# The first weight chunk of a two-layer decoder kernel: both tiles as fp32 products, loaded in 256 KB pieces on two queues

## The chip, the core and the metric

One core of one Trainium2 chip runs the whole kernel as one program. The metric is the device time of one execution in microseconds: 598.82 us is the median of three runs of the kernel before (598.73 to 599.18).

## The reference, cut to what matters

The model is a two-layer decoder trunk on 256 tokens of width 1024, all in float32. Layer 0 projects the input once, `x @ w_in`, and splits the columns: queries of a sparse attention (A), a shared key/value latent `c_kv` of 128 columns, queries, a key and weights of a small indexer, and queries, keys and values of a stick-breaking attention (B). The indexer picks 64 keys for each query.

```python
q_a, c_kv, q_idx, k_idx, w_idx, q_b, k_b, v_b = jnp.split(x @ w_in, cuts, axis=-1)
o_a = dsa_attention(q_a, rms_norm(c_kv, kv_norm), q_idx, k_idx, w_idx * IDX_HEADS ** -0.5, w_uk, w_uv)
o_b = stick_breaking_attention(q_b, k_b, v_b)
o = jnp.concatenate([o_a, o_b], axis=-1)
h = layer_norm(DEEPNORM_ALPHA * h + o @ w_out, ...)
h = layer_norm(DEEPNORM_ALPHA * h + (silu(h @ w_gate) * (h @ w_up)) @ w_down, ...)
```

Layer 1 has another attention in the same frame. The change touches only the first two tiles of `x @ w_in`: the tile of the indexer's key and weights (`k_idx`, `w_idx`), and the tile of the latent (`c_kv`).

## The kernel before

All weights come as a stream of chunks of 1 MB, 128 partitions by 2048 numbers. Chunks of the usual kind are loaded as two halves of 512 KB by SyncE (SP) into a ring of two `raw` buffers. ScalarE (ACT) rounds each half to fp32r, the high part (`split_hi_half`, into `whi`), and VectorE (DVE) subtracts to get the low part (`split_lo_half`, into `wlo`). The profile calls both `wboth`. TensorE (PE) then does three fp32r passes for each product, high by high, high by low and low by high (`HT_PASSES`), each of 128 by 256. The transposed input is `hT` (in the memory of `v`, so the profile names it `v`), with its two parts `hThi` and `hTlo` (`hTs` in the profile). A contraction over 1024 has eight tiles of 128 (`KT`).

Chunk 0 is special. It is loaded into the memory of `kT` (name `first`), and holds two tiles side by side, columns 0 to 1023 for the key and weights tile and 1024 to 2047 for the latent tile. The key and weights tile is done as plain fp32 products straight from the loaded data: 8 products, each of which the profile shows as two MATMUL records. The latent tile is done like all others, from high and low parts that ACT and DVE make by quarters (`first_quarter`), in 24 fp32r products. Ahead of the first data, PE multiplies zeros (`WARM` times, 512 columns each).

What sets the order at the start is code written out by hand for each engine. PE: zeros, key and weights tile, latent tile, chunk 1 (line 1396 and the function `cols_out`), the first half of chunk 2, transposes and the indexer's scores, and so on; from there to the end PE goes through the chunks in turn. ACT: the high parts of `hT`, of the latent tile, of chunks 1 and 2, then the copies of the first results out of PSUM, which end in `proj_evac` 1. SP issues the loads; from chunk 3 on each waits until DVE has finished with the half that it overwrites (`wlo_ready`). POOL issues the constants' load when the second half of chunk 1 has landed, and three small loads of weights when chunk 2 has.

PE reads chunk c when `wlo_ready` is 2c. The first half of chunk 2 also waits for `proj_evac` 1, and the indexer's scores for `proj_evac` 2.

Of the kernel before, what the change touches and what calls it, by code (L numbers as in the profile page):

```python
# [21 lines left out]
F32 = mybir.dt.float32  # L22
F32R = mybir.dt.float32r
ALU = mybir.AluOpType
# [3 lines left out]
P = 128  # L28
D = 1024
S = 256  # L30
KT = D // P
# [9 lines left out]
CW = 2048  # L41
# [19 lines left out]
def build(nc, x, xT, stream, w_uk, w_uv, kv_norm, ln_rows, consts, out):  # L61
    with ExitStack() as ctx:
# [3 lines left out]
        def sem(name):  # L66
            return ctx.enter_context(nc.semaphore(name))
# [4 lines left out]
        whi, wlo = wboth[:, :, 0], wboth[:, :, 1]  # L72
# [10 lines left out]
        hT = v[:].rearrange("p t (k s) -> p (t k) s", s=S)  # L83
# [11 lines left out]
        bank = [ctx.enter_context(nc.psum_tensor(f"bank{b}", [P, 512], F32)) for b in range(8)]  # L95
# [12 lines left out]
        crawT = dsel[:, 0:S]  # L108


        first = kT[:].rearrange("p k s -> p (k s)")
        FIRST = [slice(i * CW // 2, (i + 1) * CW // 2) for i in range(2)]
        QUARTER = [slice(i * CW // 4, (i + 1) * CW // 4) for i in range(4)]
# [19 lines left out]
        xT_loaded = [sem(f"xT_loaded{i}") for i in range(2)]  # L133
        first_loaded = [sem(f"first_loaded{i}") for i in range(2)]
        first_hi, first_lo = sem("first_hi"), sem("first_lo")
# [3 lines left out]
        hThi_ready, hTlo_ready = sem("hThi_ready"), sem("hTlo_ready")  # L139
# [71 lines left out]
        WARM = 10  # L211
# [65 lines left out]
        def _(sp):  # L277
            half = (slice(0, HW), slice(HW, CW))
            sp.dma_start(first[:, FIRST[0]], stream[0][:, FIRST[0]]).then_inc(first_loaded[0], 16)
            sp.dma_start(hT[:, 4:8], xT[:, 4:8]).then_inc(xT_loaded[1], 16)  # L280
            sp.dma_start(first[:, FIRST[1]], stream[0][:, FIRST[1]]).then_inc(first_loaded[1], 16)
# [17 lines left out]
            for c in range(L1_IN - 1, L1_OUT + 1):  # L299
                for j in range(2):  # L300
                    sp.wait_ge(wlo_ready, 2 * (c - RAW) + j - 1)
                    at = L1_IN + L1_ORDER[c - L1_IN] if L1_IN <= c < L1_OUT else c
# [70 lines left out]
        def _(act):  # L373
            def split_hi_half(c, j, i=0):
                act.wait_ge(raw_loaded[c % RAW][j], 16 * (c // RAW + c % RAW) + 16 * (RING // RAW) * i)
                nc.scalar.copy(whi[:, c % RING, j * HW:(j + 1) * HW], raw[:, c % RAW, j * HW:(j + 1) * HW]  # L376
                               ).then_inc(whi_ready, 1)
# [76 lines left out]
            act.dma_start(hT[:, 0:4], xT[:, 0:4]).then_inc(xT_loaded[0], 16)  # L454
            act.preload_act_table_set("natural_log_exp_and_others")
            def first_quarter(i):
                act.wait_ge(first_loaded[i // 2], 16)
                nc.scalar.copy(whi[:, 0, QUARTER[i]], first[:, QUARTER[i]]).then_inc(first_hi, 1)

            for b in range(4):  # L460
                act.wait_ge(xT_loaded[b // 2], 16)
                nc.scalar.copy(hThi[:, 2 * b:2 * b + 2], hT[:, 2 * b:2 * b + 2]).then_inc(hThi_ready, 1)
            first_quarter(2)
            first_quarter(3)
            split_hi(1)
            split_hi_half(2, 0)
            act.wait_ge(chunk_used, 1)
            nc.scalar.copy(crawT, bank[4][:, S:2 * S])
# [4 lines left out]
            split_hi_half(2, 1)  # L473
# [249 lines left out]
            for s in range(SLOTS1):  # L723
                q, half = FILL1[s]
# [24 lines left out]
        def _(dve):  # L749
# [128 lines left out]
            def first_quarter(i):  # L878
                dve.wait_ge(first_hi, i - 1)
                nc.vector.tensor_tensor(wlo[:, 0, QUARTER[i]], first[:, QUARTER[i]],  # L880
                                        whi[:, 0, QUARTER[i]].bitcast(F32), ALU.subtract).then_inc(first_lo, 1)

# [4 lines left out]
            first_quarter(2)  # L887
            first_quarter(3)
# [5 lines left out]
            for i in range(I_HEADS):  # L894
                dve.wait_ge(relu_done, i + 1)
                for t in range(2):
                    w = wq_i[:, t, i:i + 1]
# [232 lines left out]
        def _(pe):  # L1130
            mm = nc.tensor.matmul
# [239 lines left out]
            pe.wait_ge(first_loaded[0], 16)  # L1371
            for k in range(KT):
                if k % 4 == 0:
                    pe.wait_ge(xT_loaded[k // 4], 16)
                mm(bank[4][:, 0:S], first[:, k * P:(k + 1) * P], hT[:, k, :], start=(k == 0), stop=(k == KT - 1))
            for q in range(2):
                ks = range(4 * q, 4 * q + 4)
                for j, (w, a) in enumerate(HT_PASSES):
                    if j == 0:
                        pe.wait_ge(hThi_ready, 2 * q + 2)  # L1380
                        pe.wait_ge(first_hi, q + 1)
                    elif j == 1:
                        pe.wait_ge(hTlo_ready, 2 * q + 2)
                    else:
                        pe.wait_ge(first_lo, q + 1)
                    for k in ks:
                        last = mm(bank[4][:, S:2 * S], w[:, 0, (KT + k) * P:(KT + k + 1) * P], a[:, k, :],
                                  start=(k == 0 and j == 0), stop=(k == KT - 1 and j == 2))
            last.then_inc(chunk_used, 1)
            for j, (w, a) in enumerate(HT_PASSES):  # L1390
                if j == 0:
                    pe.wait_ge(whi_ready, 1)
                elif j == 2:
                    pe.wait_ge(wlo_ready, 1)
                for k in range(KT):
                    mm(bank[5][:, 0:S], w[:, 1, k * P:(k + 1) * P], a[:, k, :], start=(k == 0 and j == 0),
                       stop=(k == KT - 1 and j == 2))
# [472 lines left out]
```

## Time and profile before

| what | value |
|---|---|
| median of three runs | 598.82 us |
| the profiled execution's own time | 598.94 us |
| its span, first to last instruction | 597.2 us |
| PE busy | 589.1 us (99%) |
| PE weight load busy | 505.7 us (85%) |
| DVE busy | 424.4 us (71%) |
| ACT busy | 342.3 us (57%) |
| HBM read | 107.94 MB, 183 GB/s over the span |

The profile shows one execution. A line of instructions has the source line, the engine, the operation, what it writes and what it reads. PE's busy time is not PE at its peak, since records of pipelined matmuls overlap. The chain that ended last is followed back from the last instruction, and its entries give where the time of the end comes from. 1.74 us of the profiled execution lie outside its span.

### The profile page before, as it was taken

To read this page: it belongs to the slowest core of one execution; us is meant where nothing else is said; L and a number is where in the kernel's file an instruction comes from. 1 tells how busy PE (TensorE), PEld (TensorE's weight loads), DVE (VectorE), ACT (ScalarE), POOL (GpSimd) and SP (SyncE) were. 2 spreads that over 40 slices of the span, in tenths; PEclk is the share of its full clock that TensorE was granted. 3 is DMA by queue.
4 is the path that set the end of the run, shared out by engine and by line. 5 is a ranking of instruction groups with operands and counts; after the bars stand their busy time and mean duration, and the time that the engine had idled before them with its cause. 6 is when DMAs were issued, how large, how long until landed. Compare 5 with 4: busy or idle time off the path is not lost.

```text
span 597.2 us, 9595 instructions
## 1 busy us (share of the span) xinstructions
PE 589.1 (99%) x3354; PEld 505.7 (85%) x3354; DVE 424.4 (71%) x697; ACT 342.3 (57%) x645; POOL 26.6 (4%) x49
## 2 busy tenths in 40 slices
PE   8999999999999999999999999999999999999995
PEld 7988888888888888888888888888888888888885
DVE  4699877876776556655887888768677666665637
ACT  5776986456655544554556767645565555555530
POOL 1111111100000000000010000002000000000000
PEclk9999999999999999999999999999999999999999
DMA  8755437286676565564447543662767655555401
GB/s 309 265 179 194 142 124 245 91 291 202 223 223 207 193 205 181 182 205 140 143 148 270 180 141 117 205 207 80 237 217 234 210 202 165 185 186 189 140 1 70
DMA packets 30112, 109.43 MB, mean 183 GB/s; under 512 B 3376, under 2 KB 3376, under 8 KB 29952
## 3 DMA queue, kind: packets, MB, share of 16 engines
q1 hardware_dynamic: 28368, 102.25, 51.9%
q0 software_dynamic: 1568, 6.23, 3.4%
q10 hardware_dynamic: 144, 0.52, 0.2%
q8 instruction: 21, 0.34, 0.2%
q14 instruction: 11, 0.09, 0.0%
HBM read 107.94 MB, written 1.05 MB: 183 GB/s over the span
## 4 chain that ended last, share of the span: by engine, by line
PE 98%; DMA 1%; DVE 0%; DVEq 0%; issue 0%; ACT 0%; ACTq 0%
PE bank L1244 27%; PE bank L1152 24%; PE bank L1158 13%; PE bank L1694 5%; PE bank L1522 3%; PE bank L1698 3%; PE bank L1145 2%; PE bank L1222 2%; PE bank L1197 2%; PE bank L1198 2%; PE bank L1204 2%; PE bank L1339 1%; PE bank L1350 1%; PE bank L1330 1%; PE bank L1526 1%; PE bank L1501 1%
## 5 line engine op out<-in xcount | busy, mean ns | idle before, releaser
L753 DVE TENSOR_TENSOR wboth<-raw,wboth 128x1024 fp32r<-128x1024 f32 x190 | 225.3, 1223 | 44.5 <-ACT wboth L376 43.6
L376 ACT CAST wboth<-raw 128x1024 fp32r<-128x1024 f32 x190 | 191.2, 1047 | 21.6 <-DMA raw<-stream_in 20.8
L1152 PE MATMUL bank<-hTs,wboth 128*128 128x512 f32 x640 | 152.2, 390 | 0.0
L1244 PE MATMUL bank<-wboth,oThi 128*128 128x512 f32 x468 | 150.1, 392 | 0.0
L1152 PEld LDWEIGHTS bank<-hTs,wboth 128*128 128x128 f32 x640 | 118.8, 188 | 23.7
L1244 PEld LDWEIGHTS bank<-wboth,oThi 128*128 128x128 f32 x468 | 88.0, 188 | 18.3 <-issue 0.7
L1244 PE MATMUL bank<-wboth,oTlo 128*128 128x512 f32 x234 | 91.3, 390 | 0.0
L1158 PEld LDWEIGHTS bank<-hTs,wboth 128*128 128x128 f32 x640 | 81.9, 191 | 3.0
L1158 PE MATMUL bank<-hTs,wboth 128*128 128x256 f32 x640 | 83.2, 283 | 0.0
L1244 PEld LDWEIGHTS bank<-wboth,oTlo 128*128 128x128 f32 x234 | 44.0, 188 | 8.1
L654 ACT COPY kT<-bank 128x256 f32<-128x256 f32 x40 | 14.8, 371 | 58.8 <-PE bank L1158 58.7
L661 ACT CAST oThi<-scratch 128x256 fp32r<-128x256 f32 x40 | 16.3, 406 | 41.1 <-DVE scratch L1058 41.1
L1050 DVE TENSOR_TENSOR kT<-bank,kT 128x256 f32<-128x256 f32 x40 | 16.8, 420 | 31.5 <-ACT kT L654 31.5
L1053 DVE TENSOR_TENSOR kT<-bank,kT 128x256 f32<-128x256 f32 x40 | 17.0, 425 | 30.4 <-ACT kT L659 30.4
L657 ACT ACTIVATE scratch<-kT 128x256 f32<-128x256 f32 x40 | 16.7, 418 | 36.2 <-DVE kT L1050 36.2
L1694 PE MATMUL bank<-hTs,wboth 128*128 128x512 f32 x128 | 32.6, 395 | 0.0
L1061 DVE TENSOR_TENSOR oTlo<-scratch,oThi 128x256 fp32r<-128x256 f32 x40 | 17.0, 425 | 18.9 <-ACT oThi L661 18.9
L1694 PEld LDWEIGHTS bank<-hTs,wboth 128*128 128x128 f32 x128 | 23.0, 189 | 5.1 <-issue 1.0
L1058 DVE TENSOR_TENSOR scratch<-scratch,kT 128x256 f32<-128x256 f32 x40 | 17.0, 426 | 4.4 <-DVE kT L1053 1.5
L1197 PE MATMUL bank<-wboth,hTs 128*128 128x512 f32 x48 | 18.8, 392 | 0.0
L1198 PE MATMUL bank<-wboth,hTs 128*128 128x512 f32 x48 | 18.7, 391 | 0.0
L1698 PEld LDWEIGHTS bank<-hTs,wboth 128*128 128x128 f32 x128 | 17.4, 190 | 1.3
(189 smaller groups left out, 635.1 us busy)
## 6 DMA issues: line engine op xcount, KB each, us to landing
raw<-stream_in SPq DMA_DIRECT2D x190, 512.0 KB, 4.9
qT<-ln_rows_in POOLq DMA_DIRECT2D x8, 512.0 KB, 5.1
kT<-stream_in SPq DMA_DIRECT2D x2, 512.0 KB, 6.2
h<-x_in POOLq DMA_DIRECT2D x1, 1024.0 KB, 5.0
out<-h SPq DMA_DIRECT2D x4, 256.0 KB, 2.1
v<-xT_in ACTq DMA_DIRECT2D x1, 512.0 KB, 5.1
v<-xT_in SPq DMA_DIRECT2D x1, 512.0 KB, 6.6
dist<-consts_in POOLq DMA_DIRECT2D x1, 384.0 KB, 3.5
```

Source lines behind the costliest of these rows:

```text
L376: nc.scalar.copy(whi[:, c % RING, j * HW:(j + 1) * HW], raw[:, c % RAW, j * HW:(j + 1) * HW]).then_inc(whi_ready, 1)
L753: nc.vector.tensor_tensor(wlo[:, c % RING, cols], raw[:, c % RAW, cols], whi[:, c % RING, cols].bitcast(F32), ALU.subtract).then_inc(wlo_r ...
L1053: nc.vector.tensor_tensor(uful[:, t % 2], bank[tile_bank(t) + 1][:, 0:S], uful[:, t % 2], ALU.add).then_inc(usum_ready, 1)
L1058: nc.vector.tensor_tensor(aful[:, t % 2], sgate[:, t % 2], uful[:, t % 2], ALU.mult).then_inc(amul_ready, 1)
L1152: mm(dst[:], whi[:, slot, off + k * P:off + (k + 1) * P], hTs[:, k].rearrange("p j s -> p (j s)"), start=(k == 0), stop=False)
L1158: last = mm(dst[:, 0:S], wlo[:, slot, off + k * P:off + (k + 1) * P], hThi[:, k, :], start=False, stop=(k == KT - 1))
L1197: mm(dst, hThi[:, k, toks], whi[:, slots, cols], start=(k == 0), stop=False)
L1198: mm(dst, hThi[:, k, toks], wlo[:, slots, cols], start=False, stop=False)
L1244: last = mm(bank[4 + 2 * t + a][:], o[:, kts[j], t * P:(t + 1) * P], w[:, c % RING, j * D + a * 512:j * D + (a + 1) * 512], start=(start a ...
L1522: mm(dst[:], whi[:, c % RING, at + k * P:at + (k + 1) * P], hTs[:, k].rearrange("p j s -> p (j s)"), start=(k == 0), stop=False)
L1694: mm(dst[:], whi[:, c % RING, at + k * P:at + (k + 1) * P], hTs[:, k].rearrange("p j s -> p (j s)"), start=(k == 0), stop=False)
L1698: last = mm(dst[:, 0:S], wlo[:, c % RING, at + k * P:at + (k + 1) * P], hThi[:, k, :], start=False, stop=(k == KT - 1))
```

## The change

1. The latent tile is now also done as plain fp32 products from the loaded data, into bank 6. The quarters' high and low parts, two casts on ACT and two subtractions on DVE, are gone.
2. PE takes both tiles together, by pairs of contraction tiles: for pair b two products of the key and weights tile and two of the latent tile.
3. The input and the chunk land as eight transfers of 256 KB, four issued by SP and four by ACT, each with a semaphore of its own. Before, they were four of 512 KB, three by SP and one by ACT.
4. The products of zeros are 7 in place of 10.
5. On ACT the cast of the second half of chunk 2 now stands before the copies of the first results. The copy of the latent tile reads bank 6.
6. The waits for the input's high and low parts move to the first product of chunk 1.

```diff
-        WARM = 10
+        WARM = 7
...
-            sp.dma_start(first[:, FIRST[0]], stream[0][:, FIRST[0]]).then_inc(first_loaded[0], 16)
-            sp.dma_start(hT[:, 4:8], xT[:, 4:8]).then_inc(xT_loaded[1], 16)
-            sp.dma_start(first[:, FIRST[1]], stream[0][:, FIRST[1]]).then_inc(first_loaded[1], 16)
+            for i in (0, 2):
+                sp.dma_start(first[:, QUARTER[i]], stream[0][:, QUARTER[i]]).then_inc(first_loaded[i], 16)
+            for b in (2, 3):
+                sp.dma_start(hT[:, 2 * b:2 * b + 2], xT[:, 2 * b:2 * b + 2]).then_inc(xT_loaded[b], 16)
...
-            act.dma_start(hT[:, 0:4], xT[:, 0:4]).then_inc(xT_loaded[0], 16)
+            for b in range(2):
+                act.dma_start(hT[:, 2 * b:2 * b + 2], xT[:, 2 * b:2 * b + 2]).then_inc(xT_loaded[b], 16)
+            for i in (1, 3):
+                act.dma_start(first[:, QUARTER[i]], stream[0][:, QUARTER[i]]).then_inc(first_loaded[i], 16)
...
-            first_quarter(2)
-            first_quarter(3)
             split_hi(1)
             split_hi_half(2, 0)
+            split_hi_half(2, 1)
             act.wait_ge(chunk_used, 1)
-            nc.scalar.copy(crawT, bank[4][:, S:2 * S])
+            nc.scalar.copy(crawT, bank[6][:, 0:S])
...
-            split_hi_half(2, 1)
             split_hi_half(3, 0)
...
+            for b in range(KT // 2):
+                if b % 2 == 0:
+                    pe.wait_ge(first_loaded[b // 2], 16)
+                pe.wait_ge(xT_loaded[b], 16)
+                for tile in range(2):
+                    if b % 2 == 0 and tile == 1:
+                        pe.wait_ge(first_loaded[2 + b // 2], 16)
+                    for k in (2 * b, 2 * b + 1):
+                        at = (tile * KT + k) * P
+                        last = mm(bank[4 + 2 * tile][:, 0:S], first[:, at:at + P], hT[:, k, :], start=(k == 0),
+                                  stop=(k == KT - 1))
             last.then_inc(chunk_used, 1)
             for j, (w, a) in enumerate(HT_PASSES):
                 if j == 0:
+                    pe.wait_ge(hThi_ready, 4)
                     pe.wait_ge(whi_ready, 1)
-                elif j == 2:
+                elif j == 1:
+                    pe.wait_ge(hTlo_ready, 4)
+                else:
                     pe.wait_ge(wlo_ready, 1)
```

On TensorE, at the start of the program before, a row with a wait names the semaphores (`first_loaded0` and `first_loaded1` are the two halves of chunk 0, `xT_loaded0` and `xT_loaded1` those of the input):

```order
L1370 MATMUL bank<-zeros 128x512 x9
L1375 MATMUL bank<-v,kT 128x256 [waits xT_loaded0,first_loaded0]
L1375 MATMUL bank<-v,kT 128x256 x3
L1375 MATMUL bank<-v,kT 128x256 [waits xT_loaded1]
L1387 MATMUL bank<-hTs,wboth 128x256 [waits first_hi,hThi_ready]
L1387 MATMUL bank<-hTs,wboth 128x256 x3
L1387 MATMUL bank<-hTs,wboth 128x256 [waits hTlo_ready]
L1387 MATMUL bank<-hTs,wboth 128x256 [waits first_lo]
L1396 MATMUL bank<-hTs,wboth 128x256 [waits whi_ready]
```

The same place now; `first_loaded0` and `first_loaded1` are quarters of the key and weights tile, `first_loaded2` and `first_loaded3` quarters of the latent tile:

```order
L1359 MATMUL bank<-zeros 128x512 x6
L1369 MATMUL bank<-v,kT 128x256 [waits xT_loaded0,first_loaded0]
L1369 MATMUL bank<-v,kT 128x256
L1369 MATMUL bank<-v,kT 128x256 [waits first_loaded2]
L1369 MATMUL bank<-v,kT 128x256 [waits xT_loaded1]
L1369 MATMUL bank<-v,kT 128x256 x3
L1369 MATMUL bank<-v,kT 128x256 [waits xT_loaded2,first_loaded1]
L1369 MATMUL bank<-v,kT 128x256 [waits first_loaded3]
L1369 MATMUL bank<-v,kT 128x256 [waits xT_loaded3]
L1381 MATMUL bank<-hTs,wboth 128x256 [waits whi_ready,hThi_ready]
```

All 16 products of chunk 0 now read loaded data alone, behind six waits for transfers, and the first that needs ACT is chunk 1's. On ScalarE at the start, before (`raw_loaded10` and `raw_loaded11` are the halves of chunk 1, `raw_loaded00` and `raw_loaded01` those of chunk 2):

```order
L454 DMA v<-xT_in 128x1024
L455 ACT_TABLE_LOAD
L462 CAST hTs<-v 128x2x256 [waits xT_loaded0] x2
L458 CAST wboth<-kT 128x512 [waits first_loaded1] x2
L376 CAST wboth<-raw 128x1024 [waits raw_loaded00]
L468 COPY dsel<-bank 128x256 [waits chunk_used]
L472 COPY h<-bank 64x256
L376 CAST wboth<-raw 128x1024 [waits raw_loaded01]
```

And now:

```order
L454 DMA v<-xT_in 128x512 x2
L456 DMA kT<-stream_in 128x512 x2
L457 ACT_TABLE_LOAD
L460 CAST hTs<-v 128x2x256 [waits xT_loaded0]
L375 CAST wboth<-raw 128x1024 [waits raw_loaded00]
L375 CAST wboth<-raw 128x1024 [waits raw_loaded01]
L465 COPY dsel<-bank 128x256 [waits chunk_used]
L469 COPY h<-bank 64x256
```

ACT issues four transfers where it issued one, and its four copies out of PSUM stand behind the second half of chunk 2.

## Rows read from the trace of the kernel before

**Rows 1.** Chain that ended last, 0 to 60 us: start, us, what.

```profile
0.81 5.09 DMA v<-xT_in
5.90 0.14 issue
6.04 3.91 PE bank L1375 x16
9.96 3.10 PE bank L1387 x24
13.06 2.88 PE bank L1396 x24
33.12 1.73 PE bank L1428 x8
```

**Rows 2.** Waits of PE, longest first, 0 to 60 us.

```profile
PE bank L1370 <- POOL zeros L316: 1.4, 1, 1.4
PE bank L1375 <- DMA v<-xT_in: 0.6, 1, 0.6
```

**Rows 3.** Stretches: us, busy of five engines, granted clock, DMA share, GB/s.

```profile
1.39:2.00 0.61, 0.61 (x2) 0.51 (x3) 0.00 (x0) 0.61 (x1) 0.01 (x1) 1.00 0.16 54
2.00:3.00 1.00, 1.00 (x4) 0.81 (x3) 0.00 (x0) 0.54 (x1) 0.00 (x0) 1.00 0.58 143
3.00:4.00 1.00, 1.00 (x4) 0.81 (x3) 0.00 (x0) 0.00 (x0) 0.00 (x0) 1.00 0.97 397
4.00:5.00 1.00, 1.00 (x4) 0.77 (x4) 0.00 (x0) 0.00 (x0) 0.00 (x0) 1.00 1.05 426
8.00:10.00 2.00, 1.99 (x10) 1.46 (x9) 1.42 (x3) 1.88 (x4) 0.00 (x0) 1.00 1.02 414
```

**Rows 4.** DMA issues of 0.5 to 1.2 us and at the end: KB, us to landing.

```profile
v<-xT_in ACTq DMA_DIRECT2D x1, 512.0 KB, 5.1
kT<-stream_in SPq DMA_DIRECT2D x1, 512.0 KB, 4.9
out<-h SPq DMA_DIRECT2D x4, 256.0 KB, 2.1
```

**Rows 5.** The last stores, 586 to 597 us in 40 slices: GB/s.

```profile
GB/s 0 0 0 0 141 380 380 52 0 0 313 417 224 0 0 0 0 0 0 0 0 0 0 0 0 0 0 0 0 0 0 0 298 380 387 395 372 75 0 0
```

**Rows 6.** Products of zeros, timelines of narrow windows: start, us, engine, line, count.

```profile
2.41 3.07 PE L1370 MATMUL bank<-zeros 128*128 128x512 f32 x8
4.55 0.70 PE L1370 MATMUL bank<-zeros 128*128 128x512 f32 x2
```

**Rows 7.** Timeline of ACT, DVE and PE, 9 to 61 us.

```profile
9.20 1.14 ACT L458 CAST wboth<-kT 128x512 fp32r<-128x512 f32 x2
10.45 1.05 ACT L376 CAST wboth<-raw 128x1024 fp32r<-128x1024 f32 x1
11.54 3.78 DVE L753 TENSOR_TENSOR wboth<-raw,wboth 128x1024 fp32r<-128x1024 f32 x3 [0.40 <-ACT wboth L376]
11.73 1.05 ACT L376 CAST wboth<-raw 128x1024 fp32r<-128x1024 f32 x1 [0.23 <-DMA raw<-stream_in]
12.90 3.04 PE L1396 MATMUL bank<-hTs,wboth 128*128 128x256 f32 x24
13.01 1.05 ACT L376 CAST wboth<-raw 128x1024 fp32r<-128x1024 f32 x1 [0.23 <-DMA raw<-stream_in]
14.54 0.55 POOL L323 DMA_DIRECT2D kvrow<-kv_norm_in  x1 [1.84 <-DMA raw<-stream_in]
15.10 0.36 ACT L472 COPY h<-bank 64x256 f32<-64x256 f32 x1
16.57 1.23 DVE L753 TENSOR_TENSOR wboth<-raw,wboth 128x1024 fp32r<-128x1024 f32 x1 [1.25 <-ACT wboth L376]
21.16 1.05 ACT L376 CAST wboth<-raw 128x1024 fp32r<-128x1024 f32 x1 [1.71 <-DMA raw<-stream_in]
36.93 1.23 DVE L753 TENSOR_TENSOR wboth<-raw,wboth 128x1024 fp32r<-128x1024 f32 x1 [0.95 <-ACT wboth L376]
60.36 0.42 DVE L977 SCALAR_TENSOR_TENSOR qT<-bank,qT 128x256 f32<-128x256 f32 x1
60.83 1.43 PE L1522 MATMUL bank<-hTs,wboth 128*128 128x512 f32 x5
```

More of the change, by code:

```diff
@@ L111, in build @@
         first = kT[:].rearrange("p k s -> p (k s)")
-        FIRST = [slice(i * CW // 2, (i + 1) * CW // 2) for i in range(2)]
         QUARTER = [slice(i * CW // 4, (i + 1) * CW // 4) for i in range(4)]
@@ L132, in build @@
         raw_loaded = [[sem(f"raw_loaded{i}{j}") for j in range(2)] for i in range(RAW)]
-        xT_loaded = [sem(f"xT_loaded{i}") for i in range(2)]
-        first_loaded = [sem(f"first_loaded{i}") for i in range(2)]
-        first_hi, first_lo = sem("first_hi"), sem("first_lo")
+        xT_loaded = [sem(f"xT_loaded{i}") for i in range(4)]
+        first_loaded = [sem(f"first_loaded{i}") for i in range(4)]
         dist_loaded = sem("dist_loaded")
@@ L451, in norm @@
                     nc.scalar.copy(hThi[:, 2 * b:2 * b + 2, P:S], turned_pair(n, 1, b)).then_inc(hThi_ready, 1)
-            act.dma_start(hT[:, 0:4], xT[:, 0:4]).then_inc(xT_loaded[0], 16)
+            for b in range(2):
+                act.dma_start(hT[:, 2 * b:2 * b + 2], xT[:, 2 * b:2 * b + 2]).then_inc(xT_loaded[b], 16)
+            for i in (1, 3):
+                act.dma_start(first[:, QUARTER[i]], stream[0][:, QUARTER[i]]).then_inc(first_loaded[i], 16)
             act.preload_act_table_set("natural_log_exp_and_others")
-            def first_quarter(i):
-                act.wait_ge(first_loaded[i // 2], 16)
-                nc.scalar.copy(whi[:, 0, QUARTER[i]], first[:, QUARTER[i]]).then_inc(first_hi, 1)
             for b in range(4):
-                act.wait_ge(xT_loaded[b // 2], 16)
+                act.wait_ge(xT_loaded[b], 16)
                 nc.scalar.copy(hThi[:, 2 * b:2 * b + 2], hT[:, 2 * b:2 * b + 2]).then_inc(hThi_ready, 1)
-            first_quarter(2)
-            first_quarter(3)
             split_hi(1)
             split_hi_half(2, 0)
+            split_hi_half(2, 1)
             act.wait_ge(chunk_used, 1)
-            nc.scalar.copy(crawT, bank[4][:, S:2 * S])
+            nc.scalar.copy(crawT, bank[6][:, 0:S])
             nc.scalar.copy(wT, bank[4][DH:DH + I_HEADS, 0:S])
@@ L875, in norm @@
                 split_lo(NORM_CHUNK[n] + AHEAD)
[L878 to L881, printed above, removed]
             for b in range(4):
@@ L886, in _ @@
                                         hThi[:, 2 * b:2 * b + 2].bitcast(F32), ALU.subtract).then_inc(hTlo_ready, 1)
-            first_quarter(2)
-            first_quarter(3)
             for c in range(1, AHEAD):
@@ L1370, in _ @@
                 mm(bank[j % 4][:], zeros[:, 0:P], zeros[:], start=True, stop=True)
[L1371 to L1388, printed above, removed]
+            for b in range(KT // 2):
[9 more added lines that the diff above has]
+                                  stop=(k == KT - 1))
             last.then_inc(chunk_used, 1)
```

## The prediction

> **What bounds the kernel now.** I read the chain that ended last first. PE is on it from 6.04 us to almost the end, with no gap. It starts with the first load: 5.09 us of DMA from 0.81, then 0.14 us of issue, then the 8 fp32 products (3.91 us), the latent tile (3.10) and chunk 1's first tile (2.88) back to back [rows 1]. PE's waits say the same: in the first 60 us it waits for the zeros and once 0.6 us for the input, and for nothing else [rows 2]. So the end moves with the moment at which PE starts chunk 1 (12.90 us, [rows 7]), provided no later wait closes up. The whole question is when PE can start chunk 1 in the new order, and who is late after that.
>
> **The load.** What has moved by a time comes from the stretches [rows 3]: 54 GB/s over 0.61 us makes 33 KB at 2.0 us, then 143, 397 and 426 KB more in each us, so 573 KB at 4.0 and 999 KB at 5.0. The first pair of before, 1049 KB, is through at 5.12. It landed at 0.81 + 5.1 = 5.9 for the input and 0.82 + 4.9 = 5.7 for the chunk [rows 4], so a landing comes 0.6 to 0.8 us behind the bytes. The new first pair, a quarter of the chunk and a quarter of the input, is 524 KB. These bytes are through at 3.0 + (524 - 176)/397 = 3.88 us. Rows of 2 KB in place of 4 KB cost something: the stores at the end, of 256 KB with rows of 2 KB, move at 380 to 395 GB/s [rows 5] against 414 [rows 3], some 7%, 0.07 us here. With 0.77 us of lag the pair lands at 4.7. The issue of 0.14 puts the first product at 4.86 us. Bounds: 4.6 with a shorter lag; 6.04, no earlier than before, if the 5 us are latency and not bytes. I take 4.86, since the rates show that bytes fill the time from 3.0 on.
>
> The second product pair, of the latent tile, needs the second transfer of SP, which ends at the same byte as the 512 KB of before that landed at 5.7. With 7% for the rows, landing and issue, PE can go on at 5.9. The two products before it end at 4.86 + 0.86 = 5.72, so PE stands still for 0.2 us. The later transfers land with the third and fourth half MB, at 414 GB/s [rows 3] each 1.27 us behind the one before, so at about 7.2 and 8.5, or with before's pauses at up to 9.4. PE wants them at 8.5 and 9.4. They are hidden, if barely.
>
> The Trainium skill (DMA: Bandwidth & Descriptors, section Bandwidth) speaks against this part: transfers should be batched to 1 MiB or more for 75% of peak, with a fixed cost of about 2 us each. If that cost were paid one after the other, four transfers of a queue would, by its fit, need some 10 us and the last would be about 1 us late for PE, an estimate from the page. The rows speak otherwise: ACT's casts that wait for the successive 512 KB of one queue start 10.45, 11.73 and 13.01, 1.28 us apart [rows 7], which is bytes at 410 GB/s with no fixed part between.
>
> **The products.** A plain fp32 product of 256 columns shows as two records, and costs 1.73 / 4 = 0.432 us when nothing stops it (line 1428) [rows 1]. The 8 of before took 3.91 for 3.46, with a wait for the second half of the input in them. The latent tile's 24 fp32r products took 2.94 us, from 9.96 to 12.90 [rows 1, 7]. Now it is 8 fp32 products, 3.46 us: 0.52 us more on PE. So the change buys an earlier start with more PE work. From 5.9 there are 14 products, 6.05 us, and chunk 1 starts at 11.95 in place of 12.90. That is 0.95 us gained. Bounds: 16 products from 4.6 without a stop, 11.5 (gain 1.4); from 6.04, 12.95 (no gain).
>
> **The products of zeros.** Before, five starts from 2.41 to 4.55 are 0.43 us apart, and those behind come at 4.85 and about 5.1 [rows 6]. 512 columns in 0.43 us is the lower level of TensorE's clock, 1.2 GHz, although the granted clock stands at 1.00 there [rows 3]; the faster pace sets in near 4.7 us, after PE had worked from 1.39 on. Seven products end at 4.12 + 0.43 = 4.55, where ten end near 5.3 and would keep PE from the first data for 0.5 us. PE then has worked up to 0.15 us before the clock rose in before, so I expect the rise at the same time, and all fp32 products at 2.4 GHz. This is the step I can't see in a row, and its failure is a rival.
>
> **ACT and DVE.** Two casts (1.14 us) and two subtractions go. They ended at 10.34, before chunk 1's first half landed (cast at 10.45, [rows 7]), so their going brings nothing by itself: the casts of chunk 1 are set by the DMA. ACT issues three more transfers, and its table load comes some 1.3 us later, ending near 3.9, still ahead of the input. Chunk 1's first high part is ready at 11.50 [rows 7], 0.45 us before PE wants it. The new rows of 2 KB could push its landing back by 0.07 of 5 us, 0.35 us; a smoother load could bring it forward. So this wait is nearly closed and I price it at nothing, up to 0.4 us. The second half is subtracted at 11.54 + 2.5 = 14.05 and wanted at 11.95 + 2.88 = 14.83. Chunk 2 is complete at 16.57 + 1.23 = 17.80 before, and PE took it at 18.66 (12.90 plus 48 products at 0.12). It is wanted at 17.7 now. Its cast stood behind ACT's four copies; moved ahead of them it can start when it lands, near 14.5 by POOL's wait for the same transfer [rows 7], so its low part is there at about 16.8. The copies that it is moved past wait instead, and end at 15.5 + 1.5 = 17.0 in place of 15.46. PE waits for them (`proj_evac` 1) at the same 17.7: 0.7 us of room. Without this move PE would have lost 0.1 us there.
>
> **Further on.** The half chunk that ACT casts at 21.16 after 1.71 us of waiting for DMA [rows 7] doesn't come earlier, and DVE's long chain behind it (indexer, top-k) stays put in time until 35.98. There DVE idles 0.95 us for an ACT cast that follows PE [rows 7]; with PE 0.95 earlier this idle time closes exactly, and from there on DVE follows. At 60.36 DVE's addition ends at 60.78 and PE's product that needs it starts at 60.83 [rows 7], so there is no room: what DVE doesn't follow, PE loses. A gain of up to 0.95 passes, one beyond it is cut to about 1.0. Everything later is released by PE or by results of PE.
>
> **Sum.** Start of chunk 1 -0.95, waits at chunk 1, at 17.7 and at 60.8 nothing. The profiled execution's 598.94 becomes 597.99. The median shown is 0.12 below the profiled time: 598.82 - 0.95 = 597.87, say 597.9. Differences under 0.2 us can't be told from no change here, since the three runs span 0.45.
>
> **The rivals.**
> - *Chunk 1 comes late.* Its first high part becomes ready at 11.9 to 12.5, the 7% on the rows of 2 KB and a pause in the load like that between 5 and 8 us before. For it: 0.45 us of room only. Against: the bytes ahead of chunk 1 are the same 2 MB. Gain 0.4 to 0.6, 598.3.
> - *DVE takes part of it back* at 36 to 61 us, because the 21.16 cast comes later when more transfers stand together, and the top-k chain with it. Against: 0.95 us of idle time at 36.93. Gain 0.5, 598.3.
> - *It doesn't do what it says*: small transfers land no earlier than the large ones (the first data needed until 3.0 us to flow at all, [rows 3]), PE starts at 5.9, and the extra 0.52 us of PE work eat what the wait inside gave: 12.8, within 0.1 of before. 598.7.
> - *Slower: the clock.* PE stops at 4.55, starts at 4.86 and stops again. If the clock doesn't rise near 4.7 but only after as much work as it took before (1.39 to 4.7, 3.3 us), it rises at about 8.2. In these 3.3 us half the work is done, 1.65 us lost, and chunk 1 starts at 13.6: 0.7 slower, 599.5. It decides whenever the loss exceeds 0.95. Against: PE stands still for 0.5 us in all, where before it stood still for 0.56 [rows 2] and the pace behind was full.
>
> The Trainium skill (DMA: Bandwidth & Descriptors, section Issuing engines are not separate DMA queues) holds that issuing from several engines saves only the sequencer's time. By that rule the second queue brings no rate, and I counted none; the two first transfers of before, one on each queue, landed together [rows 4], which agrees.
>
> **How the numbers follow.** The forecast has 0.62, with 597.4 to 598.2 from its bounds (gain cut at 1.0 by DVE, or 1.4 if DVE also moves); chunk 1 late 0.15; DVE 0.08; no earlier landing 0.08; clock 0.07. Faster by over 0.2: 0.62 + 0.15 + 0.07 = 0.84; within 0.2: 0.09; slower 0.07. The range 597.3 to 598.75 takes in the first three cases and half of the fourth.
>
> **What would show it.** The first product of the chunk at 4.7 to 5.0, a short idle time ahead of the third, 16 products in about 7.1 us with record pairs 0.43 apart, chunk 1 at 11.8 to 12.1 with no wait, the cast of chunk 2's second half ahead of the copies, no PE wait at 17.7, DVE's idle time at 36 gone or under 0.1. Wrong would be: records 0.43 us apart each (the clock), an idle time of PE before chunk 1, or the first product at 5.5 or later.

## The result, and the profile after

The changed kernel takes 601.59 us (median of six runs, 601.27 to 602.00) against 598.82 before, a ratio of 1.0045 with a 95% interval of 1.0036 to 1.0055. It is 2.8 us slower. 0.95 us faster was predicted. The profiled execution took 602.0 us, its span is 600.2.

The chain that ended last, of the changed kernel; start, us, what. These rows answer to [rows 1]:

```profile
2.23 10.97 DMA kT<-stream_in
13.20 0.04 issue
13.24 2.86 PE bank L1369 x12
16.10 2.86 PE bank L1381 x24
36.14 1.73 PE bank L1413 x8
```

Chunk 1's tile begins at 16.10 where it began at 13.06, and the product at 33.12 now stands at 36.14. The 3.0 us are lost ahead of chunk 1, and at most some 0.1 is lost behind it. The chain hangs on a transfer of chunk 0 issued at 2.23 us that landed at 13.20.

PE's own timeline, start, us, records, and in brackets the idle time ahead with what ended it:

```profile
1.39 3.35 PE L1359 MATMUL bank<-zeros 128*128 128x512 f32 x7 [1.39 <-POOL zeros L315]
5.04 1.81 PE L1369 MATMUL bank<-v,kT 128*128 128x256 f32 x4 [0.30 <-DMA v<-xT_in]
7.87 2.86 PE L1369 MATMUL bank<-v,kT 128*128 128x256 f32 x12 [1.01 <-DMA kT<-stream_in]
11.69 1.13 PE L1369 MATMUL bank<-v,kT 128*128 128x256 f32 x4 [0.97 <-DMA kT<-stream_in]
13.24 2.86 PE L1369 MATMUL bank<-v,kT 128*128 128x256 f32 x12 [0.42 <-DMA kT<-stream_in]
```

PE starts at 5.04, close to the 4.86 of the forecast. Then it stops three times, each time for a quarter of chunk 0. (The printed idle times are those between modelled ends, which for matmuls lie late; from the starts, PE has nothing to do from about 6.7 to 7.9, 10.5 to 11.7 and 12.5 to 13.2.)

What moved in each microsecond; the last column is GB/s, the one before it the share of time in which the DMA engines were busy. The first rows answer to [rows 3]:

```profile
2.00:3.00 1.00, 1.00 (x4) 0.80 (x3) 0.00 (x0) 0.13 (x1) 0.00 (x0) 1.00 0.65 211
3.00:4.00 1.00, 1.00 (x4) 0.81 (x3) 0.00 (x0) 1.00 (x1) 0.00 (x0) 1.00 0.87 274
4.00:5.00 1.00, 0.74 (x2) 0.02 (x1) 0.00 (x0) 0.22 (x2) 0.00 (x0) 1.00 1.00 301
5.00:6.00 1.00, 0.95 (x2) 0.84 (x3) 0.42 (x1) 0.55 (x1) 0.00 (x0) 1.00 0.98 119
6.00:7.00 1.00, 0.86 (x3) 0.34 (x1) 0.27 (x1) 0.00 (x0) 0.00 (x0) 1.00 0.75 180
7.00:8.00 1.00, 0.14 (x1) 0.14 (x2) 0.00 (x0) 0.00 (x0) 0.00 (x0) 1.00 1.05 270
8.00:9.00 1.00, 1.00 (x5) 0.90 (x6) 0.27 (x1) 0.62 (x1) 0.00 (x0) 1.00 1.01 287
11.00:12.00 1.00, 0.31 (x1) 0.30 (x2) 0.22 (x1) 0.62 (x1) 0.00 (x0) 1.00 1.05 420
```

Between 3 and 10 us the load runs at 119 to 330 GB/s, where before it reached 397 and 426 between 3 and 5 and 414 between 8 and 10 (from 5 to 7 the kernel before fell to 336 and 254 too). The engines are busy for 0.75 of the time or more in each row from 3 us on, so the packets take longer. From 11 us on the rate is 420. The last transfers and their time to landing:

```profile
v<-xT_in SPq DMA_DIRECT2D x1, 256.0 KB, 10.3
kT<-stream_in ACTq DMA_DIRECT2D x1, 256.0 KB, 11.0
```

They were issued at 2.21 and 2.23 us. The low rate is only about half of the delay, as two longer stretches show:

```profile
2.00:10.30 8.30, 6.99 (x22) 4.99 (x21) 1.38 (x2) 2.52 (x3) 0.00 (x0) 1.00 0.92 250
10.30:13.20 2.90, 1.55 (x6) 0.70 (x5) 0.76 (x2) 1.23 (x2) 0.00 (x0) 1.00 1.03 410
```

By 10.3 us 2.1 MB had moved, as much as chunk 0 and the input hold. The kernel before had moved them by 8.3 us (327 GB/s from 2 us on), and its last piece landed 0.9 us after that. Here the last piece landed 2.9 us after, and 1.2 MB more moved in between. These can only be the halves of the next chunks, which SP had issued behind the quarters. From 11 to 12 us SP's queue (`q1`) moved 0.35 MB, and ACT's (`q10`), which still held quarters of chunk 0, moved 0.07 (packets, MB, share of the engines' time):

```profile
q1 hardware_dynamic: 113, 0.35, 87.5%
q10 hardware_dynamic: 37, 0.07, 17.1%
```

So about 2 us of the delay are a low rate, and about 2 us are last pieces that lag behind later loads. Two queues are not needed for this lag: with all eight transfers on one queue (below) 2.1 MB had moved by 10.1 us and the last piece landed near 12.5. Why single parts of a transfer lag isn't shown.

### The profile page after: what moved, and what is told of

It is laid out like the page before. It is cut to its first block, busy times and chain, and to the rows that moved or that the text cites. A ratio compares the mean times of both kernels' runs of the same rounds, so it can differ in the third digit from the quotient of the medians.

```text
span 600.2 us, 9573 instructions
## 1 busy us (share of the span) xinstructions
PE 590.1 (98%) x3343; PEld 505.7 (84%) x3343; DVE 423.4 (71%) x695; ACT 341.9 (57%) x643; POOL 26.6 (4%) x49
## 4 chain that ended last, share of the span: by engine, by line
PE 97%; DMA 2%; DVE 0%; ACTq 0%; DVEq 0%; issue 0%; ACT 0%
PE bank L1233 27%; PE bank L1141 24%; PE bank L1147 13%; PE bank L1679 5%; PE bank L1507 3%; PE bank L1683 3%; PE bank L1134 2%; PE bank L1211 2%; PE bank L1186 2%; DMA kT<-stream_in 2%; PE bank L1187 2%; PE bank L1193 2%; PE bank L1328 1%; PE bank L1339 1%; PE bank L1319 1%; PE bank L1511 1%
## 6 DMA issues: line engine op xcount, KB each, us to landing
kT<-stream_in ACTq DMA_DIRECT2D x2, 256.0 KB, 10.4
```

## The experiments

Three theories of the slow load: **pieces**, 2 KB taken out of every 8 KB of memory are slow to read (first called R, rows of 2 KB; later P); **queues**, two queues that both carry much hinder each other (Q); **number**, eight transfers where four stood (N). "2 MB landed" below is when the last piece of chunk 0 or the input had landed, which was 9.2 us before and 13.2 in the changed kernel. All times are medians, beside the kernel before on the same chip.

### Four transfers of 512 KB, two on each queue

```diff
-        WARM = 7
+        WARM = 10
...
-            for i in (0, 2): ...  for b in (2, 3): ...
+            for i in range(2):
+                sp.dma_start(first[:, i * 1024:(i + 1) * 1024], ...).then_inc(first_loaded[i], 16)
...
-            for b in range(2): ...  for i in (1, 3): ...
+            for b in range(2):
+                act.dma_start(hT[:, 4 * b:4 * b + 4], xT[:, 4 * b:4 * b + 4]).then_inc(xT_loaded[b], 16)
...
```

PE waits for the halves in place of the quarters.

> Changed kernel, but chunk 0 and the input land as four transfers of 512 KB with rows of 4 KB, two on each queue, and 10 products of zeros. Theory R (rows of 2 KB, read slowly from memory, cost the time): the load is as before, all 2 MB landed by about 9.2 us, PE starts near 5.9 and chunk 1's tile starts at 12.8 to 13.0; time 598.7 to 599.0. Theory Q (two queues that both carry a lot at once hinder each other): all 2 MB land after 11 us, chunk 1 starts at 14.5 or later; 600.5 or more. Theory N (the number of transfers in flight): half the number, so as R.

Measured: 600.50 us, ratio 1.0032 (1.0022 to 1.0042). The load is smooth; stretches of this run:

```profile
5.00:6.00 1.00, 1.00 (x3) 0.30 (x1) 0.00 (x0) 0.00 (x0) 0.00 (x0) 1.00 1.03 402
6.00:7.00 1.00, 0.88 (x3) 0.80 (x3) 0.32 (x1) 0.97 (x2) 0.00 (x0) 1.00 1.05 430
```

2 MB landed at 8.7 us, with two queues carrying 1 MB each, so queues as such are not slow. Nor is the step of 8192 bytes from row to row slow by itself: each transfer here reads 4 KB at every such step. The time came out 1.5 us above the expected range for another reason. PE's order by pairs needs the latent tile after four records, and as a whole half it landed at 8.4:

```profile
8.40 6.31 PE L1367 MATMUL bank<-v,kT 128*128 128x256 f32 x28 [0.46 <-DMA kT<-stream_in]
```

So the order by pairs is bound to small transfers: with large ones it waits.

### All eight on SP's queue

```diff
+            for i, b in ((0, 0), (2, 1), (1, 2), (3, 3)):
+                sp.dma_start(first[:, QUARTER[i]], ...).then_inc(first_loaded[i], 16)
+                sp.dma_start(hT[:, 2 * b:2 * b + 2], ...).then_inc(xT_loaded[b], 16)
```

> Changed kernel, with all eight 256 KB transfers issued by SP in the order in which PE wants them. Theory Q: the load is smooth again, 2 MB by 9.5 us, 599 or less. Theory R: rows of 2 KB are slow on one queue as well, 2 MB landed after 12 us, 601 to 602. Theory N: the first pair lands later by one issue (0.45 us), and the load stays slow, 601 to 602.

Measured: 601.03 us, ratio 1.0031 (1.0018 to 1.0043); 2 MB landed near 12.5, and the slow stretch is there:

```profile
5.00:6.00 1.00, 1.00 (x4) 0.56 (x4) 0.55 (x1) 0.42 (x1) 0.00 (x0) 1.00 0.74 160
6.00:7.00 1.00, 0.79 (x5) 0.68 (x4) 0.15 (x1) 0.00 (x0) 0.00 (x0) 1.00 0.75 156
```

Here one queue moves 160 and 156 GB/s where two moved 119 and 180, so the theory of queues falls.

### Eight transfers of 64 partitions, with rows of 4 KB

```diff
+            for r in range(2):
+                rows = slice(64 * r, 64 * r + 64)
+                sp.dma_start(first[rows, 0:1024], stream[0][rows, 0:1024]).then_inc(first_loaded[r], 16)
...
```

ACT's four transfers and the other two of SP are cut the same way, and there are 10 products of zeros.

> Changed kernel, with eight transfers of 256 KB on the same two queues, each of 64 partitions and rows of 4 KB in place of 128 partitions and rows of 2 KB; 10 products of zeros, since both halves must have landed. Theory R: packets of 4 KB as before, 2 MB by about 9.3 us, 598.7 to 599.2. Theories Q and N: same queues and number, so slow as the changed kernel, 601 or more.

Measured: 607.39 us, ratio 1.0139 (1.0122 to 1.0156). This doesn't separate the theories, since these transfers into 64 partitions ran at a rate of their own, some 220 GB/s, steady over 8 us:

```profile
4.00:8.00 4.00, 1.45 (x5) 0.78 (x4) 0.00 (x0) 0.89 (x2) 0.00 (x0) 1.00 1.04 223
8.00:12.00 4.00, 2.05 (x4) 1.18 (x4) 1.29 (x2) 0.87 (x2) 0.00 (x0) 0.51 1.03 219
12.00:16.00 4.00, 3.32 (x8) 2.72 (x9) 2.27 (x3) 2.96 (x4) 0.50 (x1) 0.50 1.02 405
```

The granted clock, the third column from the right, shows what waiting can cost on top: after PE had been busy 1.45 of the 4 us before, it stood at 0.51 and 0.50, the 1.2 GHz level, for the next 8 us.

These rows too lie 8192 bytes apart. The run with four transfers of 512 KB read 4 KB pieces of them at 402 and 430 GB/s into 128 partitions, which speaks for the partitions as the limit, but no run has 64 partitions with another step.

### Four transfers of 512 KB made of rows of 2 KB

```diff
+            sp.dma_start(first4[:, :, 0], chunk4[:, :, 0]).then_inc(first_loaded[0], 16)   # quarters 0 and 2
+            sp.dma_start(hT4[:, :, 1], xT4[:, :, 1]).then_inc(xT_loaded[1], 16)
...
```

ACT issues the other two in the same form, and there are 10 products of zeros.

> Changed kernel, with four transfers of 512 KB, each two pieces with rows of 2 KB (the first with quarters 0 and 2 of the chunk), two on each queue; 10 products of zeros. Theory R: as slow as the changed kernel, 2 MB landed near 13 us, 601 to 602. Theory N: half the transfers, 599. Theory Q: slow, as it is with 4 KB rows on two queues.

Measured: 601.79 us, ratio 1.0043 (1.0028 to 1.0057). The time is the one that theory R gave, but not for its reason: 385 and 416 GB/s between 5 and 7 us, 2 MB landed at 9.9. Rows of 2 KB as such are read fast when both 2 KB pieces of an 8 KB row are in the same transfer. PE lost its time because its first data came only at 7.2 us, after 1.2 us of waiting, and its records were slow for some 3 us behind that (3 of them from 8 to 9 us, 7 from 11 to 12), although the granted clock is printed as 1.00 there. So "rows of 2 KB" was too wide, and "number" and "pieces" stayed.

### The same eight transfers, each from contiguous memory

```diff
+    arrays["chunk0_in"] = arrays["stream_in"][0].reshape(P, 4, CW // 4).transpose(1, 0, 2)
...
-        "xT_in": xx.T.reshape(KT, P, S).transpose(1, 0, 2),
+        "xT_in": xx.T.reshape(4, 2, P, S).transpose(0, 2, 1, 3),
...
-                sp.dma_start(first[:, QUARTER[i]], stream[0][:, QUARTER[i]]).then_inc(first_loaded[i], 16)
+                sp.dma_start(first[:, QUARTER[i]], chunk0[i]).then_inc(first_loaded[i], 16)
```

> Changed kernel with the same eight transfers of 256 KB on the same two queues, but each quarter lies in one contiguous 256 KB of memory, in place of rows of 2 KB every 8 KB. Theory P (a 2 KB piece out of every 8 KB is read slowly): the load is smooth, 2 MB landed by about 9.3 us, chunk 1's tile starts near 12.0, time 597.7 to 598.3, what was predicted for the changed kernel. Theory N (eight transfers where four stood, whatever the layout): slow again between 4.5 and 10 us, 2 MB landed near 13, time 601 to 602.

Measured: 598.43 us (598.03 to 599.11), ratio 0.9995 (0.9986 to 1.0005). It is 3.2 us faster than the changed kernel, and 2 MB landed at 8.8. Against the kernel before the interval takes in 1, so it isn't shown to be faster than that one:

```profile
5.00:6.00 1.00, 1.00 (x5) 0.59 (x4) 0.55 (x1) 0.20 (x1) 0.00 (x0) 1.00 1.04 395
6.00:7.00 1.00, 1.00 (x6) 0.89 (x5) 0.55 (x1) 0.41 (x1) 0.00 (x0) 1.00 1.06 406
7.00:8.00 1.00, 1.00 (x7) 0.87 (x6) 0.43 (x2) 0.62 (x1) 0.00 (x0) 1.00 1.06 414
```

The number is the same, so the theory of number falls. It is where the pieces lie in memory. (2.1 MB had moved by 7.8 us, and the last piece landed 1.0 us after that, so the lag of the changed kernel is gone too.) PE's timeline is now the one predicted, or better, up to 45 us:

```profile
4.48 7.30 PE L1369 MATMUL bank<-v,kT 128*128 128x256 f32 x32
11.43 3.22 PE L1381 MATMUL bank<-hTs,wboth 128*128 128x256 f32 x24
45.28 1.66 PE L1507 MATMUL bank<-hTs,wboth 128*128 128x512 f32 x6 [0.42 <-ACT v L388]
```

The first product of chunk 1 starts 1.47 us earlier than before, and PE is 1.28 us ahead from 14.49 us to about 44. At 45.28, where the row shows a wait for ACT, it is only 0.7 ahead (45.99 before), and from 135 us to the end 0.8. The chain that ended last runs through this wait, back over POOL, DVE and ACT to a load of half a chunk that landed at 21.46:

```profile
13.73 7.73 DMA raw<-stream_in
```

That is the load of which the prediction said that it doesn't come earlier. The span is 0.9 us shorter (596.3). This profiled execution took 598.05 and is among the fastest of its ten.

### 10 products of zeros in the changed kernel

```diff
-        WARM = 7
+        WARM = 10
```

> Changed kernel with 10 products of zeros in place of 7. Theory load (transfers alone cost the time): the clock rises near 4.7 us as before, the first products run fast, but the last quarter still lands near 13 us, so 601.3 to 602.0, no change. Theory clock (the slow first products cost it): 1 us or more faster, 600.5.

Measured: 602.06 us, ratio 1.0057 (1.0041 to 1.0074), no faster than the changed kernel. Its first four records take 1.02 us and no longer 1.81, so the clock was up, but PE still waits for the last quarter:

```profile
5.19 1.02 PE L1369 MATMUL bank<-v,kT 128*128 128x256 f32 x4
13.27 2.86 PE L1369 MATMUL bank<-v,kT 128*128 128x256 f32 x12 [0.41 <-DMA kT<-stream_in]
```

### The transfers alone, in the kernel before

The kernel before with the eight transfers of the changed kernel, its products waiting for the quarters.

```diff
-            pe.wait_ge(first_loaded[0], 16)
...
-                    pe.wait_ge(xT_loaded[k // 4], 16)
+                    pe.wait_ge(first_loaded[k // 4], 16)
+                if k % 2 == 0:
+                    pe.wait_ge(xT_loaded[k // 2], 16)
```

> Kernel before with the changed kernel's transfers alone (eight of 256 KB on two queues); products, zeros and casts as before. Theories P and N alike: the last quarter of chunk 0 lands near 13 us, its cast and subtraction follow, and chunk 1's tile starts 3 to 4 us later than before: 601.8 to 603. If the load is slow only because of how the changed kernel uses it: 598.8.

Measured: 603.45 us, ratio 1.0069 (1.0049 to 1.0089), with 2 MB landed at 13.2 as in the changed kernel. The transfers alone make the kernel slow, without any of the new products. The runs lie between 602.05 and 604.83; in the profiled one, the slowest, the granted clock was 0.54 from 10 to 14 us and 0.50 from 14 to 17, behind PE's waits. The two runs above 604 show a mean granted clock of 0.992 and 0.993, those at 602.05 and 602.43 show 0.997, which suggests that some 3.4 us of the 4.6 come without it.

### The fp32 products alone, in the kernel before

```diff
-            for q in range(2): ...   # 24 fp32r products of the latent tile, by high and low parts
+            pe.wait_ge(first_loaded[1], 16)
+            for k in range(KT):
+                last = mm(bank[4][:, S:2 * S], first[:, (KT + k) * P:(KT + k + 1) * P], hT[:, k, :], ...)
```

> Kernel before with its four transfers of 512 KB and 10 products of zeros, the latent tile as 8 fp32 products behind the key and weights tile. By 0.432 us a product, 3.46 us stand where 2.94 stood: 0.5 us slower, 599.3 to 599.4. If the casts and subtractions of the quarters had been in the way of chunk 1: 598.8 or less.

Measured: 599.00 us, ratio 1.0002 (0.9992 to 1.0011). The latent tile took 3.45 us in the chain against 3.10, but the tile ahead of it took 3.69 against 3.91, so chunk 1 started at 13.09 where it had started at 13.06, and the time moved by less than can be told. The products are not what cost 2.8 us.

### A pitch that is no power of two, and one of 4 KB

```diff
+    arrays["chunk0_in"] = np.pad(arrays["stream_in"][0], ((0, 0), (0, 128)))      # 8704 bytes a row; 16: 8256
...
+    arrays["chunk0_in"] = arrays["stream_in"][0].reshape(P, 2, CW // 2).transpose(1, 0, 2)   # 4096 bytes a row
```

(The input is laid out the same way in each.)

> Changed kernel, with rows of memory 8704 bytes apart in place of 8192 for chunk 0 and the input, pieces of 2 KB as before. Theory alias (a pitch of a power of two sends all engines to the same part of memory): smooth load, 2 MB by 9.3 us, 598 to 599. Theory gaps (it is the reading of 2 KB out of every 8 KB itself): slow as with the changed kernel, near 13 us, 601 to 602.

> Changed kernel, rows of memory 8256 bytes apart (8192 plus 64) in place of 8192; 8704 apart was smooth. If any pitch that is no power of two does: smooth, 2 MB by 9.4 us, 598.4 to 599. If the pad has to shift the rows by more than 64 bytes to spread them: slow between 4.5 and 10 us, 2 MB near 13, 601 to 602.

> Changed kernel, with rows of memory 4096 bytes apart, each transfer reading 2 KB of every 4 KB. If the loss grows with the share of memory skipped: between the two, 2 MB landed by 9.5 to 11 us, 598.5 to 600. If any gap costs as much: near 13 us, 601 to 602.

Measured: 598.50 us with 8704 bytes from row to row (ratio 0.9995, 0.9985 to 1.0005), 598.60 with 8256 (0.9992, 0.9982 to 1.0003), and 599.19 with 4096 (1.0006, 0.9996 to 1.0016). One stretch of each, in this order:

```profile
5.00:6.00 1.00, 1.00 (x3) 0.89 (x4) 0.49 (x1) 0.47 (x1) 0.00 (x0) 1.00 1.08 416
```

```profile
5.00:6.00 1.00, 1.00 (x4) 0.77 (x4) 0.51 (x1) 0.46 (x1) 0.00 (x0) 1.00 1.01 365
```

```profile
5.00:6.00 1.00, 0.99 (x4) 0.50 (x2) 0.69 (x1) 0.01 (x1) 0.00 (x0) 1.00 0.90 221
```

The pieces are 2 KB with the same gaps in the padded kernels, and 64 bytes more from row to row bring back the full rate. So it is not the gap either. It is the step of 8192 bytes between the rows, when a transfer reads only 2 KB at each: with two such pieces, or with 4 KB, at each step the rate was 385 to 430 between 5 and 7 us in the two runs with four transfers of 512 KB. (4 KB at each step is not always enough: the kernel before, with three of its four transfers on SP's queue, fell to 336 and 254.) Half the step, 4096 bytes, costs part of the rate (221), and the last piece landed at 10.4 us.

In all these kernels chunk 0 also lies in a tensor of its own, no longer at the head of the weights' stream. No run has this with rows 8192 bytes apart. But the kernel with 4096 has it and is slow for a while, and the one with two pieces in a transfer is fast without it, so the place of the tensor is an unlikely cause.

### The kernel before, from contiguous memory

```diff
-            sp.dma_start(first[:, FIRST[0]], stream[0][:, FIRST[0]]).then_inc(first_loaded[0], 16)
+            sp.dma_start(first[:, FIRST[0]], chunk0[0]).then_inc(first_loaded[0], 16)
...
```

> Kernel before, with each of its four 512 KB transfers read from contiguous memory in place of 4 KB out of every 8 KB. If before's slow stretch between 5.5 and 7.3 us comes from that pitch: 2 MB landed by 8.6 in place of 9.17 us and PE starts chunk 1 up to 0.3 us earlier, 598.5 to 598.7. If not: 598.8, no change.

Measured: 598.09 us (597.86 to 598.56), ratio 0.9987 (0.9977 to 0.9996). It has the lowest median of all versions and is the only one whose whole interval lies below the kernel before; against the changed kernel's 598.43 from contiguous memory the intervals overlap. The slow stretch of before, in the first row here, is gone in the second:

```profile
6.00:7.00 1.00, 0.96 (x5) 0.89 (x6) 0.42 (x1) 1.00 (x2) 0.00 (x0) 1.00 0.98 254
6.00:7.00 1.00, 1.00 (x5) 0.83 (x4) 0.82 (x2) 0.88 (x3) 0.00 (x0) 1.00 1.08 438
```

2 MB landed at 8.0 in place of 9.2, and PE waits for no transfer: the chain starts with the products of zeros.

### The other contiguous kernels

> Kernel before with the changed kernel's eight transfers (the run that took 603.45), but each read from contiguous memory. Theory alias (only where the pieces lie in memory is at fault, not their number, size or queue): 5 us come back, PE starts chunk 1 at 12.0 to 12.4, 598.0 to 598.5. If eight transfers cost the kernel before something by themselves: 599.5 or more.

Measured for the kernel before with eight contiguous transfers: 598.85 us, ratio 0.9998 (0.9988 to 1.0007). Against 603.45 with the rows 8192 bytes apart, 4.6 us came back by the layout alone. The 598.0 to 598.5 that was expected did not come: chunk 1 started at 12.91, as in the kernel before.

The same eight with the changed kernel's products and `WARM = 10`:

> The contiguous quarters with 10 products of zeros in place of 7. Theory clock (what is missing to the predicted gain is a late rise of the clock after only 7 products of zeros): the spread of 1.1 us over the runs shrinks and the median falls to 598.0 to 598.2. Theory cover (10 zeros end near 5.3 us, 0.8 us after the first data): the early start is given up, 598.5 to 598.9.

Measured: 598.84 us (598.16 to 599.49), ratio 0.9998 (0.9988 to 1.0007). More zeros don't help: PE's last product of zeros is over at 6.0 in this run, the first product of chunk 0 starts at 5.83, and the early landing at 4.2 is given up. Chunk 1 starts at 12.77.

An attempt at what is given back at 45 us, with the contiguous quarters:

```diff
             evac_proj(1, 1, qiT)
-            split_hi_half(3, 1)
...
+            split_hi_half(3, 1)
             for i in range(I_HEADS):
                 act.wait_ge(dots_done, i + 1)
```

> The contiguous quarters, and on ACT the cast of chunk 3's second half moved behind the indexer's small operations (constants' cast, index weights, two squares) and ahead of its four ReLUs. In the run with contiguous quarters ACT stood 2.78 us waiting for that half (landed 21.46), and DVE's chain behind it then held PE back by 0.42 us at 45.28. Theory D (PE's gain beyond 1 us is lost to DVE's chain, whose start hangs on that load): the ReLUs start about 0.8 us earlier, PE no longer waits at 45, 0.3 to 0.5 us faster than with the contiguous quarters alone: 597.9 to 598.1. Rival (something else holds PE there): no change, 598.4.

Measured: 598.74 us (598.08 to 599.22), ratio 0.9997 (0.9988 to 1.0007), no gain. In the profiled run PE started chunk 1 at 12.40, 1 us later than in the other, and ACT now waited for PE instead:

```profile
21.86 0.18 ACT L475 ACTIVATE small<-bank 128x8 f32<-128x8 f32 x1 [2.32 <-PE bank L1391]
23.38 1.64 ACT L486 ACTIVATE scratch<-bank 128x384 f32<-128x384 f32 x4
```

The ReLUs started at 23.38, no earlier than the 23.31 of the contiguous kernel, and PE still waited 0.2 us at 45. The experiment is inconclusive: the start of the kernel varies by more than it was to show.

## Why the prediction was wrong

**The step that failed** is this one of the load: "The later transfers land with the third and fourth half MB, at 414 GB/s [rows 3] each 1.27 us behind the one before, so at about 7.2 and 8.5, or with before's pauses at up to 9.4." The last of them landed at 13.2. Some 2 us of this are the rate, 250 GB/s from 2 to 10.3 us, and some 2 us are last pieces that landed 2.9 us behind the bytes, where the prediction counted 0.6 to 0.8. The rate that I took from before was that of pieces of 4 KB, half of each row of memory. The only rows with pieces of 2 KB were stores [rows 5], to rows 4 KB apart and in the other direction, and they carried the whole price of smaller pieces, 7%. The pitch (the step from row to row) of 8192 bytes in memory was in the code, in both the input and the chunk, and I did not weigh it. The kernel with contiguous quarters and those with a padded row differ from the changed one only in how chunk 0 and the input lie in memory, and there the load lands at 8.8, 9.3 and 9.1.

**The first pair** came close, in part by luck: its bytes were through near 4.1 for the 3.9 worked out, it landed at 4.7 and 4.9, and the first product started at 5.04 for 4.86. The rate was lower than assumed here too (274 GB/s from 3 to 4 us against 397 before), but more had moved ahead of it (211 from 2 to 3 us against 143). From contiguous memory the pair landed at 4.0 and 4.2. The second transfers, expected at 5.7 to 5.9, came at 7.8 and 8.1; this alone held PE up by 2 us.

**The products** came as priced where data were there: from 13.24 us 12 records passed until PE's next line started at 15.75, 2.51 us where 6 products by 0.432 make 2.6. In the kernel with fp32 alone the latent tile took 3.45 us for the 3.46 worked out. That the whole kernel lost only 0.2 us by it, within what can be told, leaves this term neither shown nor refuted in the end time.

**The clock.** I expected the rise near 4.7 us also with 7 products of zeros. In the profiled run the first four records took 1.81 us where four at full pace take 0.86, so it came later. This cost nothing, as PE waited for data behind it, and 10 products of zeros brought nothing. The rival of a slower kernel by the clock had the right sign by the wrong mechanism. Such a loss exists, though: in the two slowest experiments PE's waits were followed by 7 to 10 us at the lower level.

**The rival "chunk 1 comes late"** named the right cause in one half sentence, a pause in the load and dearer rows of 2 KB, with a price of 0.4 us at most for what was 4 us. The room at the wait for chunk 1 was never used: ACT's cast was late because everything was late.

**The move of chunk 2's cast, and the waits at 17.7 us.** The changed kernel says little of them, since it came there 3 us late: PE waits for nothing behind 13.24 us, and the later rows are those of before, shifted by 2.9 to 3.2 us. With contiguous quarters PE was 1.28 us ahead at this place and did not wait either, so the room was there.

**DVE's room of 0.95 us.** In the changed kernel this idle time stands unchanged, since DVE moved with PE. With contiguous quarters DVE had no idle time ahead of this subtraction, and PE, 1.28 us ahead until then, was 0.7 ahead from 45.28 on and 0.8 at the end. So the limit of about 1.0 us that was predicted for 60 us is there, but it is tighter and closes already at 45 us. The median gain of that kernel is only 0.4 us and within what can't be told from none; its runs spread over 1.1 us, and in the four profiled runs with a full rate and 7 products of zeros chunk 1 starts anywhere from 11.4 to 12.4. How much of the rest is the load and how much the time at which the clock rises is open.

**Small slips** that change nothing in the forecast: between 2.41 and 4.55 us there are six starts 0.43 us apart, not five, and the chances of its three cases "faster by over 0.2" add up to 0.85, not 0.84.

What it is in the memory that dislikes the step of 8192 bytes isn't shown by these runs. They show that step, piece and rate only.

## What to carry to other kernels

When a transfer is cut into smaller pieces of the free dimension, its rows in memory keep their old pitch. Look at the bytes per row and the pitch before taking a rate from larger transfers, and have the host lay each piece out contiguously, or pad the rows, if the pitch is a power of two (8192 bytes was the costly one here). Better still, try the layout by itself first: here it made the kernel before faster by 0.7 us, while the finer waits and the new products showed no gain beyond that even from contiguous memory. A first landing 1.0 us earlier was worth nothing when the last came 4 us later. And the margin of a hidden transfer (here 0 to 0.9 us) belongs into the range with the price of the least known rate in it.

## What the runs showed of the hardware

- Reading 2 KB pieces from rows 8192 bytes apart ran at 119 and 180 GB/s between 5 and 7 us of the start. With rows 8256 bytes apart it was 365 and 406, with 4096 bytes 221 and 363, contiguous 395 and 406. Two 2 KB pieces of each row in one transfer ran at 385 and 416. 4 KB pieces 8192 bytes apart ran at 336 and 254 there with three transfers on SP's queue and one on ACT's, at 402 and 430 with two on each, and contiguous at 397 and 438.
- Of the slow load, the last piece landed 2.9 us after as many bytes had moved as the transfers hold (13.2 and 10.3 us), where it was 0.9 before and 1.0 from contiguous memory.
- The Trainium skill (DMA: Bandwidth & Descriptors, Latency and other measured facts) tells of copies within the chip's memory with rows at large powers of two apart: at 512 KiB, the smallest listed, it gives 207 GB/s, at 4 and 8 MiB 103, and with a pad of 4 KiB on the 4 MiB the full 214, while a pad of 192 bytes did not help. Here, in loads with pieces of 2 KB, the rate fell at a pitch of 8 KiB, and a pad of 64 bytes was enough. The measurement decides for this case.
- The Trainium skill (DMA: Bandwidth & Descriptors, Bandwidth) advises to batch transfers to 1 MiB or more for 75% of peak, by measurements of transfers that GpSimd issued. The prediction's estimate from it, four transfers of a queue one after the other in some 10.4 us, begins at the issue at 0.8 us, so the last would have been 1.8 us late for PE and not about 1. The advice is not borne out as a limit for transfers queued here by SP and ACT: eight contiguous transfers of 256 KB ran at 379 to 414 GB/s between 4 and 8 us. Larger ones still landed sooner: 2 MB at 8.0 us in four of 512 KB, against 8.8 in eight, both from contiguous memory.
- Transfers into 64 partitions in place of 128, of 4 KB pieces 8192 bytes apart, ran at 219 to 223 GB/s on two queues, about half the 402 and 430 into 128, with the DMA engines busy all the time.
